# A mixture-of-experts tail: last expert and second choices summed by TensorE in PSUM, choice rows zeroed in the trunk and read behind the last weights

## What is computed

```
e_val, e_idx = lax.top_k(e_sel, EXPERT_TOP_K)            # two choices of a token
e_w = jax.nn.softmax(e_val, axis=-1) * g_val
for e in range(N_EXPERTS):
    y = (jax.nn.silu(t @ w_gate[e]) * (t @ w_up[e])) @ w_down[e]
    out = out + combine[:, e:e + 1] * y
x = x + out
return rmsnorm(x, norm_final_g)
```

## Time and profile before

| | us |
|---|---|
| median of 3 runs | 896.89 (896.64 to 898.61) |
| the profiled execution | 898.12 |
| its span | 896.4 |
| TensorE busy in the span | 821.6 (92%) |
| VectorE busy | 331.9 (37%) |
| ScalarE busy | 200.0 (22%) |
| GpSimd busy | 155.6 (17%) |

### The profile page before, as it was taken

How to read it: one execution, slowest core, us unless ns; L and a number is a source line. 1 busy time by engine, 2 the same in 40 slices (tenths; PEclk the granted TensorE clock), 3 DMA queues, 4 the chain that set the end, 5 groups by cost and what they waited for, 6 DMA issues and landing times.

```text
span 896.4 us, 15462 instructions
## 1 busy us (share of the span) xinstructions
PE 821.6 (92%) x5319; PEld 567.6 (63%) x5320; DVE 331.9 (37%) x616; ACT 200.0 (22%) x295; POOL 155.6 (17%) x241
## 2 busy tenths in 40 slices
PE   7999999999999999998998999999989999978850
PEld 6888887888888888894554554455545555534420
DVE  4799997841645246257111101110011110110107
ACT  4633435142643223141000000000000000000003
POOL 4232901000320000010311122112211222211100
PEclk8999999999999999999999999999999999999985
DMA  8693321824234938559999999999999999999976
GB/s 260 132 202 98 101 88 20 176 86 126 71 117 167 419 118 321 218 200 350 405 421 420 420 421 421 427 421 425 422 422 424 420 425 422 427 424 420 422 306 245
DMA packets 71744, 265.19 MB, mean 296 GB/s; under 512 B 29526, under 2 KB 30550, under 8 KB 54516
## 3 DMA queue, kind: packets, MB, share of 16 engines
q1 hardware_dynamic: 65428, 254.10, 74.5%
q0 software_dynamic: 6128, 10.45, 3.1%
q10 hardware_dynamic: 144, 0.02, 0.0%
HBM read 256.59 MB, written 16.52 MB: 305 GB/s over the span
## 4 chain that ended last, share of the span: by engine, by line
PE 80%; DMA 6%; DVE 5%; SPq 4%; issue 2%; ACT 2%; POOL 0%; DVEq 0%; POOLq 0%; ACTq 0%
PE ps L1070 36%; PE ps L465 23%; PE ps L481 12%; DMA slot_x<-in_exp_w_gate 5%; SPq L448 3%; PE ps L1055 2%; PE ps L471 1%; DVE pair L709 1%; DVE pair L704 1%; DMA ssm<-choice_rows 1%; PE ps L1047 1%; DVE hl L754 1%; PE ps L591 1%; PE ps L1220 0%; PE ps L1213 0%
## 5 line engine op out<-in xcount | busy, mean ns | idle before, releaser
L704 DVE TENSOR_TENSOR pair<-pair,ps 128x256 f32<-128x256 f32 x32 | 13.5, 420 | 334.5 <-PE ps L465 334.5
L1070 PE MATMUL ps<-h_hi,w_hi 128*128 128x512 f32 x280 | 109.2, 390 | 0.0
L1070 PE MATMUL ps<-h_hi,w_lo 128*128 128x512 f32 x280 | 109.0, 389 | 0.0
L1070 PE MATMUL ps<-h_lo,w_hi 128*128 128x512 f32 x280 | 108.9, 389 | 0.0
L1504 DVE TENSOR_TENSOR w_lo<-raw,w_hi 128x1024 fp32r<-128x1024 f32 x56 | 72.5, 1296 | 95.6 <-ACT w_hi L1308 94.9
L1308 ACT CAST w_hi<-raw 128x1024 fp32r<-128x1024 f32 x59 | 61.8, 1050 | 188.5 <-PE ps L1070 188.5
L465 PE MATMUL ps<-ssm,pair 128*64 128x256 f32 x832 | 94.6, 384 | 4.9 <-DMA ssm<-in_exp_w_gate 4.2
L465 PEld LDWEIGHTS ps<-ssm,pair 128*64 128x64 f32 x832 | 61.4, 139 | 42.2 <-issue 15.2
L768 ACT COPY late<-ps 128x512 f32<-128x512 f32 x35 | 20.5, 586 | 297.9 <-PE ps L481 297.9
L852 POOL DMA_INDIRECT choice_rows<-late,put_now x35 | 35.5, 1015 | 291.7 <-ACT late L768 242.2
L1070 PEld LDWEIGHTS ps<-h_hi,w_lo 128*128 128x128 f32 x280 | 52.6, 188 | 11.0
(11 more groups left out here) (341 smaller groups left out, 1205.7 us busy)
## 6 DMA issues: line engine op xcount, KB each, us to landing
ssm<-in_exp_w_gate SPq DMA_DIRECT2D x16, 2048.0 KB, 23.3
raw<-in_w_in SPq DMA_DIRECT2D x40, 512.0 KB, 4.2
au<-in_exp_w_up SPq DMA_DIRECT2D x8, 2048.0 KB, 26.1
ssm<-in_exp_w_up SPq DMA_DIRECT2D x8, 2048.0 KB, 21.9
ssm<-in_exp_w_down SPq DMA_DIRECT2D x8, 2048.0 KB, 23.1
hl<-in_exp_w_down SPq DMA_DIRECT2D x8, 2048.0 KB, 26.3
slot_x<-in_exp_w_gate SPq DMA_DIRECT2D x8, 2048.0 KB, 29.7
raw<-in_exp_w_down SPq DMA_DIRECT2D x8, 2048.0 KB, 28.5
```

Of the source, the lines that this page charges most:

```text
L704: nc.vector.tensor_tensor(act_cols, silu_cols, up_now, ALU.mult).then_inc(act_ready, 1)
L1070: t = nc.tensor.matmul(bank, lhs, rhs, start=k == 0 and n == 0, stop=k == 2 * count - 1 and n == 2)
```

## The change

1. In the trunk SyncE writes zeroes over all of `res_d` (4 MB), from 64 partitions that hold zeroes; GpSimd waits for it before the experts.
2. The last expert's results are not stored. The reads of chosen rows wait only for the stores of experts 30 and 29 (`res_stored`), and for second blocks; where a token chose expert 31 the row read is zero.
3. VectorE makes, in the tables and before the expert loop, `last_hot`: for each token tile a 128x128 matrix with a token's weight in the column of its slot in expert 31's list.
4. Behind the last down product TensorE turns `last_hot` into a PSUM bank, VectorE copies it, and makes `second_diag`, four diagonals of second-choice weights. TensorE then multiplies expert 31's rows into all eight PSUM banks (two products over 64 partitions for each tile), and on top of them each tile's second-choice rows by its diagonal; for tile 3 the residual too.
5. VectorE adds first choices from SBUF as before and one PSUM result for each tile, in a new order. ScalarE loads the root's table before the sums.
6. The loop over further `over` bodies stands inside the test whether there is any. Some semaphores are merged.

```diff
+        last_hot = [pwrev[:].rearrange("p r j q -> p (r j q)")[:, P * i:P * (i + 1)] for i in range(2)] + [
+            rw[:].rearrange("p k n -> p (k n)")[:, P * i:P * (i + 1)] for i in range(2)]
+        last_hotT = xg[1].rearrange("p (i t) -> p i t", i=NT)
+        second_diag = slots[EW[2]["down"]][:, 0:NT * P].rearrange("p (i t) -> p i t", i=NT)
+        last_chosen = stat[:, 32:40].rearrange("p (c i) -> p c i", c=2)
+        last_by_choice, last_pos, last_weight = stat[:, 0:8], stat[:, 40:44], stat[:, 44:48]
...
-            with eng.Fori(1, NOV) as o_:
-                with eng.If(n > o_):
-                    body(o_, False)
+                with eng.Fori(1, NOV) as o_:
+                    with eng.If(n > o_):
+                        body(o_, False)
...
+                sp.wait_ge(res_stored[b], (NE // 2 - b) * 16)
...
-            each_over(pe, over)
...
+            n = each_over(pe, over)
+
+            pe.wait_ge(merge_ready, 1)
+            for i in range(NT):
+                t = nc.tensor.transpose(ps[:, B_HOT, P * i:P * (i + 1)], last_hot[i], ident[:])
+            t.then_inc(merged, 1)
+            with pe.If(n > 0):
+                pe.wait_ge(ov_act, n * OV_ACT)
+                pe.sem_inc(passed, 1)
+            flag, before = second_of(pe, NE - 1)
+            pe.wait_ge(res2_ready, before + flag + 1)
+            pe.wait_ge(xgT_ready, NE + 1)
+            pe.wait_ge(res_ready, NE)
+            pe.wait_ge(merge_ready, 2)
+            for i in range(NT):
+                for c in range(2):
+                    at = slice(CAP * c, CAP * (c + 1))
+                    nc.tensor.matmul(ps[:, 2 * i + c], last_hotT[at, i], res[1][at], start=True, stop=False)
+            for i in range(NT):
+                if i == NT - 1:
+                    pe.wait_ge(tail_in, 16 * 2)
+                    for c in range(2):
+                        nc.tensor.matmul(ps[:, 2 * i + c], ident[:], x3_end[:, i, W * c:W * (c + 1)], start=False, stop=False)
+                pe.wait_ge(picked[i][1], 16)
+                for c in range(2):
+                    t = nc.tensor.matmul(ps[:, 2 * i + c], second_diag[:, i], picked_rows(i)[:, D + W * c:D + W * (c + 1)],
+                                         start=False, stop=True)
+                t.then_inc(merged, 1)
+
...
+            v.wait_ge(merged, 1)
+            nc.vector.tensor_copy(last_hotT.rearrange("p i t -> p (i t)"), ps[:, B_HOT])
+            v.wait_ge(done["down"], NE)
+            for i in range(NT):
+                made = nc.vector.tensor_scalar(second_diag[:, i], ident[:], wts[:, NT + i:NT + i + 1], None, ALU.mult)
+            made.then_inc(merge_ready, 1)
...
-                nc.vector.reciprocal(stat[:, 24 + i:25 + i], stat[:, 20 + i:21 + i]).then_inc(fin_step, 1)
-                v.wait_ge(fin_step, i + 1)
+                then(nc.vector.reciprocal(stat[:, 24 + i:25 + i], stat[:, 20 + i:21 + i]))
...
-            for i in range(NT):
-                for c in range(2):
-                    v.wait_ge(picked[i][c], 16)
-                    nc.vector.scalar_tensor_tensor(x3_end[:, i], picked_rows(i)[:, D * c:D * (c + 1)], wts[:, NT * c + i:NT * c + i + 1], x3_end[:, i],
-                                                   ALU.mult, ALU.add).then_inc(sums_ready, 1)
-                    v.wait_ge(sums_ready, 2 * i + c + 1)
-
-                if i >= 1:
-                    final_norm(i - 1)
-            final_norm(NT - 1)
+            def first_choice(i, onto):
+                v.wait_ge(picked[i][0], 16)
+                return nc.vector.scalar_tensor_tensor(x3_end[:, i], picked_rows(i)[:, 0:D], wts[:, i:i + 1], onto,
+                                                      ALU.mult, ALU.add)
+
+            def onto_residual(i):
+                then(first_choice(i, x3_end[:, i]))
+
+            def merge(i):
+                by_tensor = ps[:, 2 * i:2 * i + 2].rearrange("p c n -> p (c n)")
+                v.wait_ge(merged, i + 2)
+                if i < NT - 1:
+                    nc.vector.tensor_tensor(x3_end[:, i], x3_end[:, i], by_tensor, ALU.add).then_inc(sums_ready, 1)
+                else:
+                    first_choice(i, by_tensor).then_inc(sums_ready, 1)
+
+            onto_residual(0)
+            onto_residual(1)
+            merge(0)
+            merge(1)
+            onto_residual(2)
+            final_norm(0)
+            merge(2)
+            final_norm(1)
+            merge(3)
+            final_norm(2)
+            final_norm(3)
...
+            nc.scalar.activation(stat[:, 62:63], eps, ACT.Sqrt)
...
+                act.wait_ge(sums_ready, i + 1)
...
+            gp.wait_ge(rows_zeroed, 16)
...
             gp.wait_ge(xt_full, NE - 1)
             fetch(NE, 0, NE - 2, xg_in[0], idx_copied, 0)
             second_fetch(NE - 1)
+            first_put(NE - 2, 0, NE // 2 - 1)
             for e in range(NE - 2, NE):
-                first_put(e, e % 2, e // 2)
                 second_put(e)
             gp.wait_ge(xt_full, NE + 1)
...
             load_units(13, 25)
-
+            sp.wait_ge(pool_made, MADE["bs"])
+            sp.dma_start(res_d.rearrange("(n p) w -> p n w", p=P // 2),
+                         bs_split[P // 2:P].bitcast(F32).rearrange("p h t -> p (h t)").unsqueeze(1)
+                         .to_broadcast((P // 2, 4 * T // (P // 2), W))).then_inc(rows_zeroed, 16)
...
+            for c, m in enumerate((M1, M2)):
+                mark(vv.tensor_copy(last_chosen[:, c].unsqueeze(2), m[:, :, NE - 1:NE]))
+            mark(vv.tensor_scalar(last_pos.unsqueeze(2), pos[:, :, NE - 1:NE], -1.0, float(CAP - 1), ALU.mult, ALU.add))
...
+            then(mul(last_by_choice, last_chosen.rearrange("p c i -> p (c i)"), wts[:]))
+            then(add(last_weight, last_by_choice[:, 0:NT], last_by_choice[:, NT:2 * NT]))
+            for i in range(NT):
+                made = vv.tensor_scalar(last_hot[i], slot_iota, last_pos[:, i:i + 1], last_weight[:, i:i + 1], ALU.is_equal, ALU.mult)
+            made.then_inc(merge_ready, 1)
+            experts_vector(v, then)
```

More of the change, by code:

```diff
@@ L339, in trunk @@
         onehot_ready, exp_in, exp_out = (sem(n) for n in ("onehot_ready", "exp_in", "exp_out"))
-        hot_ready, block_ready = sem("hot_ready"), sem("block_ready")
+        slot_tables = sem("slot_tables_ready")
+        rows_zeroed, merge_ready, merged = sem("choice_rows_zeroed"), sem("merge_operands_ready"), sem("merged_by_tensor")
         second_rows = sem("second_rows_moved")
@@ L343, in trunk @@
         rows1_full, rows1_copied = sem("rows1_full"), sem("rows1_copied")
-        rows0_copied = [sem(f"rows0_copied{n}") for n in range(2)]
+        rows0_copied = sem("rows0_copied")
         out_stored, tail_in, sums_ready, outrow_ready = (
             sem(n) for n in ("out_stored", "tail_in", "sums_ready", "outrow_ready"))
-        fin_step = sem("fin_step")
         passed = sem("passed")
@@ L418, in trunk @@
                  "down": exp_w_down[0].rearrange("e (h p j) n -> e p h (j n)", p=P, j=2)}
-        B_XT, B_AT, B_GATE, B_UP, B_RES, B_RES2 = 0, 1, 2, 3, (6, 7), 4
+        B_XT, B_AT, B_GATE, B_UP, B_RES, B_RES2, B_HOT = 0, 1, 2, 3, (6, 7), 4, 5
         xt_bank = ps[:, B_XT].rearrange("p (j r) -> p j r", j=4)
@@ L566, in experts_sync @@
             for b in range(2):
-                sp.wait_ge(res_stored[b], NE // 2 * 16)
+                sp.wait_ge(res_stored[b], (NE // 2 - b) * 16)
             for i in range(NT):
@@ L598, in experts_tensor @@
             pick(place1, B_RES[1], range(2))
-            for half in range(2):
-                pe.wait_ge(rows0_copied[half], 1)
+            pe.wait_ge(rows0_copied, 2)
             for j in range(4):
@@ L610, in experts_tensor @@
             hidden(xgT, 0, "up", B_UP).then_inc(done["up"], 1)
-            pe.wait_ge(hot_ready, 1)
-            pe.wait_ge(block_ready, 1)
+            pe.wait_ge(slot_tables, 2)
             taken(pe, ("rt", 2, 1))
@@ L695, in experts_tensor, with experts_vector @@
             pe.wait_ge(ov_ready, 1)
-            each_over(pe, over)
-        def experts_vector(v):
+            n = each_over(pe, over)
[25 more added lines that the diff above has]
+                t.then_inc(merged, 1)
+        def experts_vector(v, then):
             def turn(e, first):
@@ L785, in experts_scalar @@
             act.wait_ge(rows0_full, 1)
-            nc.scalar.copy(rows0[:, 0:2 * P], ps[:, B_XT, 0:2 * P]).then_inc(rows0_copied[0], 1)
-            act.wait_ge(rows0_copied[0], 1)
-            nc.scalar.copy(rows0[:, 2 * P:W], ps[:, B_XT, 2 * P:W]).then_inc(rows0_copied[1], 1)
+            nc.scalar.copy(rows0[:, 0:2 * P], ps[:, B_XT, 0:2 * P]).then_inc(rows0_copied, 1)
+            act.wait_ge(rows0_copied, 1)
+            nc.scalar.copy(rows0[:, 2 * P:W], ps[:, B_XT, 2 * P:W]).then_inc(rows0_copied, 1)
             act.wait_ge(rows1_full, 1)
-            act.wait_ge(hot_ready, 1)
+            act.wait_ge(slot_tables, 1)
```

(10 more changed lines are left out.)

## The result

The change makes the kernel **slower by 1.44%**: 911.11 us median (910.03 to 911.8, 4 runs) against 896.76 us for the kernel before in the same session (896.39 to 898.61, 4 runs); ratio 1.0144, 95% interval 1.0128 to 1.0161. The forecast was 892.3 us in a range of 889.5 to 896.2. It was wrong in sign: said -4.6 us, measured +14.3. The profiled execution took 911.6 us with a span of 909.9, so the spans show 909.9 - 896.4 = 13.5 of it.

A forecast was written before the change was run, and what follows sets the result against it. It took TensorE to set the trunk, the weight stream the middle, and a 31.1 us tail the end; -6.0 in the tail and +1.4 before it gave -4.6, from 896.89 to 892.3 us, range 889.5 to 896.2.

The forecast's parts named there:

- The zeroes ... nothing: Trunk: the 4.19 MB write takes 10 to 12.5 us under 20 us of idle DMA cover, costing nothing.
- Rival D: Trunk: zero write holds SyncE or slows code and table loads, +3 to +8 us, 896 us in all; 4%.
- Behind the down product (865.3): four transposes: Tail: TensorE turns the last expert's matrix right behind the last down product, 0.9 us, ending at 866.2.
- Eight products ... 3.6 us: Tail: eight 64-partition products of the last expert's rows, array halves side by side, 3.6 us, ending at 871.6.
- rival A: Tail: TensorE merges at half clock, eight products 7.2 us, 3.6 us per tile; 902.5 us in all; 5%.
- What it costs before ... +1.4: Before expert 0's product: six VectorE instructions delay it and expert 4's weight load, +1.4 us, bounds 0.5 to 2.0.
- Reads behind the last weights: Tail: eight reads wait only for expert 30's put (859.9), take 10 us, landing 870.7 to 879.4.
- rival B: Tail: reads still end by 884, tail gain only 2 to 2.5 us, 895.9 us in all; 8%.
- VectorE's tail: Tail: seven wide steps and four reciprocal-gain pairs end at 887.4, plus 3.0 store; gain 6.0 us, bounds 3.0 to 7.5.

The follow-up runs named there:

- zero_middle: The changed kernel with its one 4 MB zero write read from partitions 32 to 95 instead of 64 to 127: 903.74 us, ratio 1.0061.
- no_jump: The changed kernel with TensorE's sums directly behind the expert loop and the overflow code behind them: 901.92 us, ratio 1.0049.
- middle_late_no_jump: The changed kernel with zeroes read from partitions 32 to 95, last expert's tables behind expert 0's turn, sums ahead of overflow code: 894.52 us, ratio 0.9955.
- three_mends: The changed kernel with zeroes in eight pieces, last expert's tables behind expert 0's turn, sums ahead of overflow code: 893.0 us, ratio 0.9953.
- zero_split: The changed kernel with the zeroes written in eight 512 KB pieces behind weight units 36 to 43: 903.29 us, ratio 1.0053.
- tables_late: The changed kernel with VectorE's six instructions for the last expert's tables moved behind expert 0's turn: 905.87 us, ratio 1.0087.
- reads_wait: The changed kernel with SyncE issuing the eight reads of chosen rows only after TensorE's four transposes: 908.86 us, ratio 1.0125.
- before_zero: The kernel before with only the one 4 MB zero write and GpSimd's wait for it added: 904.65 us, ratio 1.0083.
- last_group_peeled: The changed kernel with TensorE's last four experts written out behind its loop, the jump over overflow code kept: 909.61 us, ratio 1.0133.
- all_four: The changed kernel with zeroes in eight pieces, late tables, sums ahead of overflow code, last four experts written out: 892.88 us, ratio 0.9949.

## Why the prediction was wrong

- **"The zeroes ... nothing"** is the first step that failed: +6.7 us in the trunk of this profile (5.2 to 5.8 in five others with the same write), 7.2 on the whole time when alone on the kernel before. The cover of the earlier trace rows was read as a cover of bandwidth. It was sound for SyncE, less so for TensorE, whose code comes over the same DMA engines: the row's 0.01 share held that code, and nothing else. The rate was wrong by half as well, 197 GB/s instead of 336 to 420 (the prediction named half the rate, but saw in it only a delay of the next loads); zero_middle shows that at the rate assumed the step would have cost nothing. Rival D named "slows code and table loads in the trunk: +3 to +8" and got 4%. It was the case that came, with its price.
- **"Behind the down product (865.3): four transposes"** is the second: it lets TensorE start at once. It sat 6.75 us. Nothing in the trace of before could show the price, since TensorE had no work behind the overflow code there; the jump was in the listing, though, and a path that is new on an engine needed a bound from both sides like any cost that no row shows.
- **"Eight products ... 3.6 us"** was right in the pairing of halves: 3.70 and 3.71 us in no_jump and middle_late_no_jump. In the change they took 6.50, as the clock had fallen: it was 0.86 from 880 to 882, in the stall, and 0.50 when TensorE went on. The stall isn't needed for it: three_mends has none, and they took 5.40. That is rival A's mechanism, at its place, with 2.9 us for the eight; the tile products then ran at full clock (3.70 us for two tiles, against 7.2 in A), so the half clock did not last as A had it.
- **"What it costs before ... +1.4"** had the 1.4 us right (1.42 by the rows) and its effect too small. The pause of TensorE grew from 1.47 to 2.88 us, and expert 0's down product took 2.1 us more at the lower clock, ahead of the load on which the stream hangs; the hole in the DMA windows is 4 us wide. The sum took each instruction's time and let all products run at full clock. Of these 2.1 us only 0.7 went with the tables (5.78 to 5.11); the placing products' 1.7 us were in no term either. What slows them is open.
- **"Reads behind the last weights"** was right: they were issued when expert 30's put had landed (864.77 + 6.58 = 871.35), 5.1 us ahead of the down product's end (5.4 forecast), and the DMA engines stayed full until 9.5 us behind it (9.7 forecast). Only the landings were mis-sized a little. In no_jump VectorE has tile 0's first choice 5.6 us behind that end (5.4 forecast) and tile 1's 9.0 us behind it (7.9 forecast), and TensorE waits 1.19 us for tile 1. It is rival B's mechanism at a smaller price: the tail's 25.8 instead of 25.1.
- **"VectorE's tail"** of 6.0 us was right once the rest was mended: 31.1 - 25.7 = 5.4 us in three_mends, 5.3 in no_jump. It was hidden in the change behind TensorE, whose first tile VectorE awaited for 6.16 us.

With the three mends the time is 893.0 us, close to the 892.3 forecast for the change. That the two are so close is partly luck: the tables' 1.4 us are in the forecast and not in three_mends, while its profile has 1.7 us at the placing products and 1.3 at expert 0's down product that the forecast had not. But the tail's gain was there (5.4 us of 6.0), and the costs that the sum had put at nothing outweighed it.

## What to carry to other kernels

Look at what an engine's instruction stream needs before putting work on it or a transfer beside it: code behind a skipped block costs 5 to 7 us at first use if nothing has brought it in, so keep the path that is taken in line, and the rare one behind it. A bulk DMA in an idle stretch can hold back an engine's code: here it was free in pieces, and free in one write that ran at full rate from partitions on both sides of 64. Where TensorE feeds what a stream hangs on, ask of each pause what the products behind it would cost at the lower clock.

## What was not expected of the hardware

- A jump over code not run costs TensorE 5.17 us with the DMA engines running empty (share 0.57, then 0.10), and 5.46 to 6.75 with them full, against 0.47 to 0.72 for going straight on. It goes on 2.6 us behind the landing of a code packet.
- A 4 MB write beside TensorE held it for 3.7 us in one place and 0.7 in another; at 385 GB/s and all but over by 141 us it held it nowhere.
- The same 4 MB in the same packets: 197 GB/s from partitions 64 to 127, 385 from 32 to 95.
- Whether the granted clock falls in a pause of 0.6 to 1.8 us differs from one kernel to the next with the same instructions. The 16 placing records took 3.65 us in the kernel before, zero_split, tables_late, reads_wait, no_jump and zero_middle, and 5.03 to 5.35 in the change, before_zero, last_group_peeled, three_mends, all_four and middle_late_no_jump, all behind pauses of 1.7 and 0.6 us. Expert 0's down product took 3.65 us in the kernel before and 4.72 in before_zero, behind the same 1.5 us. What decides it stays open; throwaway transposes in the pauses kept it at 1.00 in both kernels that had them.
